# The prompt's first two query blocks of each head column are scored, normalised and summed as one block

## What is computed

```python
proj = jnp.einsum('bsd,de->bse', rmsnorm(x, norm_g), w_in)        # q, k, v, g_a, u, v_s, g_b, m_a, m_b
# prompt attention: 8 heads of 64; with 512 rows and a top 3 of past blocks every query sees all its past
s = einsum('qhd,hkd->hqk', q / 8, k) + table[h, rel_bucket(pos_q - pos_k)]     # -inf where pos_k > pos_q
out = einsum('hqk,hkd->qhd', softmax(s), v)
y_a = out * silu(g_a)
...
# sample attention: each sequence over 16 cached pages of 128 rows, top 3 of 8 blocks by q.mean(k)
return x + (sigmoid(m_a) * (y_a @ w_pa) + sigmoid(m_b) * (y_b @ w_pb)) @ w_o   # then the final rmsnorm
```

## Time and profile before

| | |
|---|---|
| median of 3 runs | 599.32 us (597.98 to 601.37) |
| the profiled execution | 598.01 us, its span 595.9 us |
| TensorE busy (matmul) | 574.4 us, 96% of the span |
| VectorE busy | 312.3 us, 52% |
| ScalarE busy | 213.0 us, 36% |
| granted TensorE clock | 0.997 of full speed over the span |

### The profile page before, as it was taken

One profiled execution on the slowest core, in us unless ns is written; L12 is line 12 of the kernel. 1 busy time (PEld: TensorE's weight loads), 2 busy tenths in 40 slices (PEclk: granted clock), 3 DMA queues, 4 the chain that ended last, 5 costly groups with the idle time before them and its releaser, 6 DMA issues.

```text
span 595.9 us, 15270 instructions
## 1 busy us (share of the span) xinstructions
PE 574.4 (96%) x6260; PEld 538.7 (90%) x6260; DVE 312.3 (52%) x693; ACT 213.0 (36%) x467; POOL 27.5 (5%) x39
## 2 busy tenths in 40 slices
PE   7999999999999999999999989999999989999993
PEld 5999999998889899899889978998989989999992
DVE  5633324336448446656856654884362373692316
ACT  5422223325334433444544341332342231242242
POOL 2101112000000000000000000120000000000002
PEclk9999999999999999999999999999999999999998
DMA  8447424665685675766758568785789566323003
GB/s 265 123 161 231 126 95 150 206 184 172 199 246 173 215 232 171 251 189 211 223 161 265 178 216 261 242 257 174 247 281 307 191 203 223 113 74 122 21 1 150
DMA packets 74888, 111.91 MB, mean 188 GB/s; under 512 B 5418, under 2 KB 39219, under 8 KB 74820
## 3 DMA queue, kind: packets, MB, share of 16 engines
q1 hardware_dynamic: 73588, 107.59, 57.1%
q0 software_dynamic: 1232, 3.36, 2.0%
HBM read 106.39 MB, written 4.53 MB: 186 GB/s over the span
## 4 chain that ended last, share of the span: by engine, by line
PE 81%; DVE 11%; ACT 3%; issue 2%; DMA 1%; SPq 0%; POOL 0%; DVEq 0%; ACTq 0%; POOLq 0%
PE BK L475 45%; PE BK L620 8%; PE BK L495 7%; PE BK L632 4%; PE BK L646 4%; PE BK L556 2%; PE BK L696 2%; DVE WL L1061 1%; PE BK L713 1%; PE BK L703 1%; DMA SGC<-in_gating_constants 1%; ACT SC L952 1%; DVE NMX L1253 1%; ACT APX L965 1%; PE BK L672 1%
## 5 line engine op out<-in xcount | busy, mean ns | idle before, releaser
L475 PE MATMUL BK<-XH,WH 128*128 128x272 f32 x672 | 212.7, 316 | 0.0
L475 PE MATMUL BK<-XH,WL 128*128 128x272 f32 x672 | 194.2, 289 | 0.0
L475 PE MATMUL BK<-XL,WH 128*128 128x272 f32 x672 | 193.2, 288 | 0.0
L475 PEld LDWEIGHTS BK<-XH,WH 128*128 128x128 f32 x672 | 126.6, 188 | 9.9 <-issue 8.7
L475 PEld LDWEIGHTS BK<-XL,WH 128*128 128x128 f32 x672 | 127.2, 189 | 0.0
L475 PEld LDWEIGHTS BK<-XH,WL 128*128 128x128 f32 x672 | 126.5, 188 | 0.0
L1061 DVE TENSOR_TENSOR WL<-WRAW,WH 128x1024 fp32r<-128x1024 f32 x59 | 72.2, 1223 | 87.6 <-ACT WH L847 87.4
L620 PE MATMUL BK<-CST,KRAW 128*128 128x128 f32 x512 | 77.1, 273 | 2.4 <-DVE ATS L1238 2.2
L1158 DVE COPY KT<-BK 128x512 f32<-128x512 f32 x64 | 44.2, 690 | 57.1 <-PE BK L620 56.7
L847 ACT ACTIVATE WH<-WRAW 128x1024 fp32r<-128x1024 f32 x60 | 63.2, 1054 | 21.3 <-PE BK L495 21.3
L620 PEld LDWEIGHTS BK<-CST,KRAW 128*128 128x128 f32 x512 | 60.2, 140 | 4.5 <-issue 4.1
(11 more groups left out here) (196 smaller groups left out, 804.4 us busy)
## 6 DMA issues: line engine op xcount, KB each, us to landing
KRAW<-in_cache_k SPq DMA_DIRECT2D x128, 256.0 KB, 3.3
VRAW<-in_cache_v SPq DMA_DIRECT2D x120, 256.0 KB, 3.8
WRAW<-in_w_in SPq DMA_DIRECT2D x21, 1024.0 KB, 5.7
WRAW<-in_w_o SPq DMA_DIRECT2D x4, 1024.0 KB, 5.2
XR<-in_x_prompt SPq DMA_DIRECT2D x4, 512.0 KB, 6.3
VEX<-in_cache_v SPq DMA_DIRECT2D x8, 256.0 KB, 4.3
WRAW<-in_w_pb SPq DMA_DIRECT2D x4, 512.0 KB, 6.5
WRAW<-in_w_pa SPq DMA_DIRECT2D x4, 512.0 KB, 4.9
```

Source lines behind the costliest of these rows:

```text
L475: last = mm(BK[h][:, 0:HALF], w[:, n % 2, k, :], x[:, k, cols], start=(i == 0 and w is WH and x is XA), stop=(i == KC - 1 and w is WL))
```

## The change

Blocks 0 and 1 of each head column (y = 0 with 128 keys and y = 1 with 256) become one block of 384 columns in the same banks. The list of blocks is now 12 long, ((0,1), (2), (3)) for each of four head columns, and the prompt's work ends at step 66 in place of 82. No arithmetic is added or dropped. Each piece and head keeps its own maximum, exponential, accumulator and scale; what is merged are the copies, the reciprocal, the negation, the gate and all waits.

```diff
+BLOCKS = [(c, ys) for c in range(PAIRS) for ys in ((0, 1), (2,), (3,))]
+def parts(i):
+    ys = BLOCKS[i][1]
+    starts = [0, P] if len(ys) == 2 else [0]
+    return [(x, y, o, (y + 1) * P) for x, (y, o) in enumerate(zip(ys, starts))], sum(y + 1 for y in ys) * P
...
             def prompt_exp(i):
-                n = (i % 4 + 1) * P
                 act.wait_ge(pm_ok, i + 1)
                 wait(act, at_pe, i)
-                for e in range(2):
-                    act.activation(APX[:, e, 0:n], BK[6 + e][:, 0:n], ACT.Exp, bias=NMX[:, e:e + 1], scale=1.0 / UNIT,
-                                   accum_out=PLS[:, e:e + 1]).then_inc(ae_ok, 1)
+                for x, y, o, n in parts(i)[0]:
+                    for e in range(2):
+                        act.activation(APX[:, e, o:o + n], BK[6 + e][:, o:o + n], ACT.Exp, bias=NMX[:, 2 * x + e:2 * x + e + 1],
+                                       scale=1.0 / UNIT, accum_out=PLS[:, 2 * x + e:2 * x + e + 1]).then_inc(ae_ok, 1)
...
             def prompt_gate(i):
-                c, y = i // 4, i % 4
+                c, ys = BLOCKS[i]
...
-                g = G[:, GA + c, y * P:(y + 1) * P]
-                dve.tensor_tensor(g, BK[6][:, 0:P], g, ALU.mult).then_inc(av_ev, 1)
+                g = G[:, GA + c, ys[0] * P:(ys[-1] + 1) * P]
+                dve.tensor_tensor(g, BK[6][:, 0:len(ys) * P], g, ALU.mult).then_inc(av_ev, 1)
...
-                if t % 4 == 0 and 20 <= t < 84:
+                if t % 4 == 0 and 20 <= t < 68:
                     prompt_turn(t // 4 - 5)
-                if t % 4 == 1 and 21 <= t < 85:
+                if t % 4 == 1 and 21 <= t < 69:
                     prompt_values(t // 4 - 5)
-                if t % 4 == 2 and 18 <= t < 82:
+                if t % 4 == 2 and 18 <= t < 66:
                     prompt_scores(t // 4 - 4)
```

More of the change, by code:

```diff
@@ L64, with parts_before @@
 STEPS = 144
+BLOCKS = [(c, ys) for c in range(PAIRS) for ys in ((0, 1), (2,), (3,))]
[3 more added lines that the diff above has]
+    return [(x, y, o, (y + 1) * P) for x, (y, o) in enumerate(zip(ys, starts))], sum(y + 1 for y in ys) * P
+def parts_before(i):
+    return sum(2 * len(ys) for _, ys in BLOCKS[:i])
 def bucket(d):
@@ L225, in build @@
         NHALF = sb("NHALF", [P, 1])
-        NMX = sb("NMX", [P, 2])
-        PLS = sb("PLS", [P, 2])
+        NMX = sb("NMX", [P, 4])
+        PLS = sb("PLS", [P, 4])
         assert top[0] <= nc.sbuf_usable_end, (top[0], nc.sbuf_usable_end)
@@ L429, in _ @@
                 if t == 84:
-                    sp.wait_ge(av_ev, 16)
+                    sp.wait_ge(av_ev, len(BLOCKS))
                     sp.dma_start(WSR[:], w_s[0].rearrange("g t s -> t g s")).then_inc(sgw_ld, 16)
@@ L686, in prompt_scores @@
             def prompt_scores(i):
-                c, y = i // 4, i % 4
+                c = BLOCKS[i][0]
                 if i == 0:
@@ L690, in prompt_scores @@
                 wait(pe, av_ev, i)
-                n = (y + 1) * P
-                for k0 in range(0, n, 256):
-                    k1 = min(k0 + 256, n)
-                    for e in range(2):
-                        hd = slice(e * HD, (e + 1) * HD)
-                        last = mm(BK[6 + e][:, k0:k1], QT[hd, c, y * P:(y + 1) * P], KTS[hd, c, k0:k1], start=True, stop=True)
+                for x, y, o, n in parts(i)[0]:
+                    for k0 in range(0, n, 256):
+                        k1 = min(k0 + 256, n)
+                        for e in range(2):
+                            hd = slice(e * HD, (e + 1) * HD)
+                            last = mm(BK[6 + e][:, o + k0:o + k1], QT[hd, c, y * P:(y + 1) * P], KTS[hd, c, k0:k1], start=True, stop=True)
                 last.then_inc(ps_pe, 1)
             def prompt_turn(i):
-                pe.wait_ge(ap_ok, 2 * i + 2)
+                pe.wait_ge(ap_ok, parts_before(i + 1))
                 for e in range(2):
-                    for j in range(i % 4 + 1):
+                    for j in range(parts(i)[1] // P):
                         last = pe.transpose(BK[6 + e][:, j * P:(j + 1) * P], APX[:, e, j * P:(j + 1) * P], IDN)
@@ L706, in prompt_values @@
             def prompt_values(i):
-                c, y = i // 4, i % 4
+                c = BLOCKS[i][0]
                 pe.wait_ge(a0_ok, i + 1)
                 pe.wait_ge(a1_ok, i + 1)
[L710 to L714, removed]
+                for x, y, o, n in parts(i)[0]:
+                    for j in range(y + 1):
+                        for e in range(2):
+                            hd = slice(e * HD, (e + 1) * HD)
+                            last = mm(BK[6][hd, x * P:(x + 1) * P], VROW[:, j, c * P + e * HD:c * P + (e + 1) * HD],
+                                      APT[:, e, o + j * P:o + (j + 1) * P], start=(j == 0), stop=(j == y))
                 last.then_inc(av_pe, 1)
@@ L960, in prompt_exp @@
             def prompt_exp(i):
-                n = (i % 4 + 1) * P
                 act.wait_ge(pm_ok, i + 1)
                 wait(act, at_pe, i)
-                for e in range(2):
-                    act.activation(APX[:, e, 0:n], BK[6 + e][:, 0:n], ACT.Exp, bias=NMX[:, e:e + 1], scale=1.0 / UNIT,
-                                   accum_out=PLS[:, e:e + 1]).then_inc(ae_ok, 1)
+                for x, y, o, n in parts(i)[0]:
+                    for e in range(2):
+                        act.activation(APX[:, e, o:o + n], BK[6 + e][:, o:o + n], ACT.Exp, bias=NMX[:, 2 * x + e:2 * x + e + 1],
+                                       scale=1.0 / UNIT, accum_out=PLS[:, 2 * x + e:2 * x + e + 1]).then_inc(ae_ok, 1)
             def prompt_out(i):
-                n = (i % 4 + 1) * P
+                n = parts(i)[1]
                 act.wait_ge(at_pe, i + 1)
@@ L1002, in _ @@
                     exponentials(t // 16 - 1)
-                if t % 4 == 3 and 19 <= t < 83:
+                if t % 4 == 3 and 19 <= t < 67:
                     prompt_exp(t // 4 - 4)
-                if t % 4 == 0 and 20 <= t < 84:
+                if t % 4 == 0 and 20 <= t < 68:
                     prompt_out(t // 4 - 5)
@@ L1010, in _ @@
                 if t == 130:
-                    act.wait_ge(av_ev, 16)
+                    act.wait_ge(av_ev, len(BLOCKS))
                     act.wait_ge(pj, matmuls_before(T_PB))
@@ L1241, in prompt_max @@
             def prompt_max(i):
-                c, n = i // 4, (i % 4 + 1) * P
-                w = min(n, 2 * P)
+                c = BLOCKS[i][0]
+                m = 2 * len(BLOCKS[i][1])
                 dve.wait_ge(ps_pe, i + 1)
@@ L1246, in prompt_max @@
                     dve.wait_ge(tph_ld, 16)
[L1247 to L1250, removed]
+                for x, y, o, n in parts(i)[0]:
+                    w = min(n, 2 * P)
+                    for e in range(2):
+                        sc = BK[6 + e][:, o + n - w:o + n]
+                        bias = TPH[:, 2 * c + e, 0:w]
+                        add = dve.tensor_tensor(sc, sc, bass.AP(bias.tensor, bias.offset + w - 1, [list(bias.ap[0]), [-1, w]]), ALU.add)
                 link(add)
-                for e in range(2):
-                    top_of = dve.tensor_reduce(NMX[:, e:e + 1], BK[6 + e][:, 0:n], AX.X, ALU.max)
+                for x, y, o, n in parts(i)[0]:
+                    for e in range(2):
+                        top_of = dve.tensor_reduce(NMX[:, 2 * x + e:2 * x + e + 1], BK[6 + e][:, o:o + n], AX.X, ALU.max)
                 link(top_of)
-                dve.tensor_scalar(NMX[:], NMX[:], -1.0 / UNIT, None, ALU.mult).then_inc(pm_ok, 1)
+                dve.tensor_scalar(NMX[:, 0:m], NMX[:, 0:m], -1.0 / UNIT, None, ALU.mult).then_inc(pm_ok, 1)
             def prompt_norm(i):
[L1258 to L1262, removed]
+                m = 2 * len(BLOCKS[i][1])
+                dve.wait_ge(ae_ok, parts_before(i + 1))
+                link(dve.reciprocal(PLS[:, 0:m], PLS[:, 0:m]))
+                for x, y, o, n in parts(i)[0]:
+                    for e in range(2):
+                        dve.tensor_scalar(APX[:, e, o:o + n], APX[:, e, o:o + n], PLS[:, 2 * x + e:2 * x + e + 1], None, ALU.mult).then_inc(ap_ok, 1)
             def prompt_out(i):
-                n = (i % 4 + 1) * P
+                n = parts(i)[1]
                 dve.wait_ge(at_pe, i + 1)
@@ L1270, in prompt_gate @@
             def prompt_gate(i):
-                c, y = i // 4, i % 4
+                c, ys = BLOCKS[i]
                 dve.wait_ge(av_pe, i + 1)
-                if y == 0:
+                if ys[0] == 0:
                     dve.wait_ge(pj_ev[0], T_GA + c + 1)
                     dve.wait_ge(pj_ev[1], T_GA + c + 1)
-                g = G[:, GA + c, y * P:(y + 1) * P]
-                dve.tensor_tensor(g, BK[6][:, 0:P], g, ALU.mult).then_inc(av_ev, 1)
+                g = G[:, GA + c, ys[0] * P:(ys[-1] + 1) * P]
+                dve.tensor_tensor(g, BK[6][:, 0:len(ys) * P], g, ALU.mult).then_inc(av_ev, 1)
             def mask_mixing():
@@ L1385, in _ @@
                     page_out(t)
```

(2 more changed lines are left out.)

## The result

The changed kernel took 604.25 us against 598.65 us of the kernel before: a ratio of 1.0083 (95% interval 1.0054 to 1.0113), or 5.0 us slower (3.2 to 6.8). A second set of runs gave 603.94 against 599.55 us, ratio 1.0062 (1.0039 to 1.0085). The profiled execution took 604.81 us, its span is 602.8 us.

The account below looks back on a forecast made before the run. The prediction took TensorE's instruction list as the bound; its savings and new waits summed to +4.0 us, moving the profiled execution from 598.01 to 602.0 us and the median from 599.32 to 603.3 us, range 599.6 to 606.3 us.

Parts of the forecast that it names:

- Strips: TensorE's scores, turns and values: merging saves 0.52 us for each of four head columns, −2.1 us.
- estimate of 2.8 us: Alternative size for the strips' saving: sixteen fewer tiling-mode changes at 175 ns each; not used in the sum.
- Page turn behind PT: Steps 20, 36, 52: TensorE's page turn waits for ScalarE's copy PT, queued behind the prompt's exponentials, +3.5 us.
- Page turn behind the local part: Steps 21, 37, 53: page turn waits for VectorE's local-part reading, which stands behind the prompt's longer copy, +0.8 us.
- Steps 32 to 34: Merged block replaces y = 3 there: later exponentials and gate make TensorE wait, together +1.0 us.
- Gate at 66 and 50: TensorE's gate waits go: −0.9 us at step 66, where no scores stand, and −0.1 at step 50.
- Steps 67 and 83: Longer TensorE waits for the sample's exponentials: +1.0 us at step 67 and +0.8 at step 83.
- Only the merging counts: Rival, 10%: strips shrink by 2.1 us and the waits stay as they are, 597.2 us.
- Faster: Rival, 6%: VectorE and ScalarE, freed in steps 68 to 82, make the 0.90 and 0.94 us waits vanish, 595.3 us.
- Half-size: Rival, 16%: chains overlap better, new waits give +4.0 rather than 7.1 us, 600.3 us.
- More: Rival, 8%: delays feed on each other, late exponentials holding back evictions and weight splitting, about +3 more, 606 us.

Follow-up runs that it names:

- PT first: Changed kernel with ScalarE's copy PT done one step earlier, ahead of the prompt's exponentials: ratio 1.0027 to the kernel before.
- the edit: Changed kernel with VectorE reading the sample's local part one step earlier, ahead of the prompt's copy: ratio 1.0072 to the kernel before.
- the experiment with the large block: Kernel before, nothing merged, each head column's four pieces in reverse order, 512 columns first: ratio 1.0139 to the kernel before.
- the three edits together: Changed kernel with PT ahead of the prompt's exponentials, local part ahead of the prompt's copy, sample's exponentials ahead of the tanh: ratio 0.9944 to the kernel before.

## Why the prediction was right

The sum was +4.0 us and the changed part took +3.65 us. The medians moved by 5.6 us in the first comparison. Of the difference between the two profiled executions 2.55 us are the late start. The starts of the others were not recorded. So it is likely, and not shown, that late starts make up most of what the 5.6 us have beyond the 3.65. The sum came nearer than its terms. The strips saved 0.75 us more than predicted and the wait behind PT came out 0.3 us short, and four misses of about 0.2 us each the other way took most of that back: so much of the agreement is luck. By steps, with waits taken from starts:

- *Strips, −2.1 predicted, −2.85 measured: the term that was mis-sized.* Scores gave 1.15 and values 1.0 us, the turn nothing (0.1 the other way), much as worked out. What I missed stands one instruction later: the first filling matmul behind a strip is followed after 0.23 us and not 0.13. In the changed kernel's scores of step 34 and what follows:

```profile
199.40 0.40 PE L491 MATMUL BK<-XH,WH 128*128 128x272 f32 x1
199.64 0.29 PE L491 MATMUL BK<-XL,WH 128*128 128x272 f32 x1
199.77 0.29 PE L491 MATMUL BK<-XH,WL 128*128 128x272 f32 x1
```

  With 0.1 us on each of eight strips that are no longer there it is another 0.8. The Trainium skill (TensorEngine Tiling (Array Packing), Key Properties) says that a change of tiling mode drains TensorE, and the trace agrees in kind: into the scores, which use 64 of 128 rows, TensorE takes 0.22 us, into a page turn, which uses all of them, 0.13. But the late second filling matmul is not tied to such a change alone. It comes behind a page turn as well, after 0.20 to 0.21 us:

```profile
315.70 0.37 PE L491 MATMUL BK<-XH,WH 128*128 128x272 f32 x1
315.90 0.29 PE L491 MATMUL BK<-XL,WH 128*128 128x272 f32 x1
```

  The prediction's estimate of 2.8 us, made with the 175 ns of the Trainium skill (TensorE: Matmul & The Clock Gate, Single matmul latency), lies on the measured value, which may be chance, as no run separates the parts of a change of mode.
- *Page turn behind PT, +3.5 predicted, +3.2 measured.* 1.82, 0.80 and 1.28 us, for 1.9, 0.9 and 1.4. The chain of 4.4 us was 4.34. The kernel with PT first took 3.22 us away.
- *Page turn behind the local part, +0.8 predicted, +1.0 measured* (0.30, 0.30, 0.43), and −1.05 by the edit.
- *Steps 32 to 34, +1.0 predicted, +1.0 measured:* 0.42 us at the block sums and values of step 33, 0.66 at the gate in place of 0.12.
- *Gate at 66 and 50, −1.0 predicted, −0.8 measured.* The 0.97 of step 66 went, but that of step 50 grew from 0.12 to 0.29 instead of going: the values strip ahead of it is shorter and the gate's chain isn't, the same error as in the experiment with the large block.
- *Steps 67 and 83, +1.8 predicted, +2.0 measured:* 1.10 us, and 1.99 for 1.10.
- *Not foreseen, +0.2:* at step 70 the page turn waits 0.36 us for the sample's output (ATS), where the prompt's values had covered it; a wait of 0.18 at step 81 went.

−2.85 + 3.2 + 1.0 + 1.0 − 0.8 + 2.0 + 0.2 = +3.7 us. The rivals fall. Only the merging counts: the strips did shrink, but the waits moved by 6.5 us. Faster: the exponentials would have had to end 2.5 us after the scores, it was 4.34. Half-size: the new waits came to full size. More: no late eviction shows among the waits, and the delays hardly touched each other (the three edits together give 6.7 us, singly 6.5).

## What to carry to other kernels

In a hand-written order an instruction's price is set by what stands behind it in its own queue. Look for the copy that frees a bank for the engine that bounds the kernel, and see what is ahead of it and how long TensorE still has; here the merged block's longer chain in front of it cost 1.65 us more at step 20, over twice the 0.7 us that merging saves a head column. Taking work off the bounding engine also takes cover off every chain it hid (steps 67, 70, 83), so a saving of 2.85 us and new waits belong in one sum. And when total times scatter by nearly as much as the effect, lay the two timelines over each other at fixed marks: it gave 3.65 and 3.72 us for the same change where the medians gave 5.6 and 4.4.

## What the runs showed of the hardware that was not expected

The start of the program has two lengths. TensorE's first matmuls, kernel before:

```profile
1.60 2.93 PE L509 MATMUL BK<-VS 128*128 128x256 f32 x6 [1.60 <-DVE NHALF L1065]
4.46 2.07 PE L516 MATMUL BK<-GROW,ONE 1*128 1x512 f32 x4
```

and changed kernel:

```profile
1.60 2.93 PE L525 MATMUL BK<-VS 128*128 128x256 f32 x6 [1.60 <-DVE NHALF L1082]
4.46 3.78 PE L532 MATMUL BK<-GROW,ONE 1*128 1x512 f32 x4
```

The same four matmuls take 2.07 us in one execution and 3.78 in the other, though the instructions up to there are the same. The eight matmuls behind them differ alike, 1.99 against 3.78 us; first the kernel before, then the changed one:

```profile
6.46 1.99 PE L509 MATMUL BK<-VS 128*128 128x256 f32 x8
```

```profile
8.16 3.78 PE L525 MATMUL BK<-VS 128*128 128x256 f32 x8
```

In both executions a matmul of this kind follows the one before it after 0.43 us at first and after 0.22 us, half of that, later. The step from one to the other lies between 4 and 7 us in the first and at about 14 us in the second. It parts all twelve traces as step 0 does: the four early ones have the short spacing by 7.1 us, the eight late ones only from 13.5 to 14.5 us on. The granted clock reads 1.00 of full speed for this whole stretch in both, so the profile shows no change of the clock. That it is TensorE's clock rising from 1.2 to 2.4 GHz, later in some executions, fits the halving and is my reading; no run here sets it, and why both groups occur stays open. It is worth 1.9 to 2.6 us at step 0 against the kernel before, as much as the times scatter. That it makes most of that scatter is likely; the starts of executions that weren't profiled are not recorded. The other surprise is the 0.1 us behind each strip, told above.
